# A two-layer attention trunk on one core: the first operands of the input projections turned operand by operand between the first products, and spread factors turned by halves

## The chip, the cores and the metric

The kernel runs on one core of a Trainium2 chip. The metric is the device time of one execution in microseconds (us), taken as the median of several runs. TensorE multiplies and transposes, VectorE (DVE) and ScalarE (ACT) move and combine tiles, GpSimd (POOL) does elementwise work too and issues some DMAs, SyncE (SP) issues most of them. The engines meet only through semaphores.

## The reference

`x` has 2048 tokens of 1024 float32 values. Two layers follow each other, each with an RMS norm ahead and a residual addition behind, and a last RMS norm ends the trunk:

```python
for layer in range(DEPTH):                       # DEPTH = 2
    h = rms_norm(x, norm_g[layer])
    if layer % 2 == 0:
        u = h @ w_in_even[i]                     # 1024 x 3328
        aq, ak, av, ag, bq, bk, bv, bg = jnp.split(u, even_splits, axis=-1)
        a_out = diff_attention(...)              # 4 heads, two softmax maps each, causal by chunks of 64
        b_out = swa_sink_attention(...)          # 8 heads, window of 128, a sink per head
        mixed = jnp.concatenate([a_out * silu(ag), b_out * silu(bg)], axis=-1)
        y = mixed @ w_out_even[i]
    else:
        u = h @ w_in_odd[i]                      # 1024 x 4096
        c_out = chunk_attention(...)             # 16 heads, own chunk and the 8 before it
        y = (c_out * silu(cg)) @ w_out_odd[i]
    x = x + y
return rms_norm(x, final_g)
```

## The kernel before

The program is a row of stages with a barrier of all engines between them: `p0` (input projection of the even layer), `a` (differential attention), `b` (window attention), `o0` (output projection), `p1`, `c`, `o1` for the odd layer. Names in rows begin with the stage's letter; `p_` and `o_` stand for both projections. `share`, `share_low` and `p_operands` hold operands of the products.

**Input projection (`project`, L111).** It multiplies with seven products in place of eight (a Strassen-Winograd scheme). The 2048 tokens are taken in two passes of 1024, the columns in slabs of 256: 13 slabs in `p0`, 16 in `p1`; a pass and a slab make a group `e` of seven products, one for each operand A11, S2, S1, A12, S3, A22, S4. Each product is 12 matmuls of 128x512, since each factor is a high part (rounded, float32r) and a low part (the rest), and three of the four combinations are kept. A group writes four output blocks `n`.

A pass's operands come from four *pairs* `q` of token tiles, a pair being two tiles of 128 tokens by 1024 values. For each pair and operand (28 in all) TensorE turns a 128x512 piece by four 128x128 transposes (L967) into one of four PSUM banks used in turn, ACT writes the high part (`high`, L525), DVE the low part (`low`, L698), and only then is the bank free for the turn four places on. Four operands are sums that POOL makes (`sums_of`, L322: S1, S2, S3, S4; in `p1` DVE makes S1). In `p0` each tile is normalised first: ACT squares, DVE takes mean, inverse and scales (`mean_pair`, `invert_pair`, `scale_one`). The order of the *head*, that is of the first pass, is written out by pairs: all seven operands of pair 0, then pair 1, and so on. `HEAD` is the order inside a pair, `turn_at` the place of a turn in it. Products begin after all 28 turns.

The eight tiles of the head have six places: four in `x_buf`, and tiles 4 and 5 in the second buffer of raw weights, `raws[1]` (`LENT`); tiles 6 and 7 wait on SP until the first pair is turned. So the second slab of weights is loaded once pair 2 is turned (POOL, L287). POOL also makes the sums and low parts of the weights (L291 to L315; for group 1 DVE makes the low parts, `low_weights`, L779, while group 0 runs).

In a group, ACT copies the first product out (`first_sum`, L595), DVE adds products (`near_sum` L879, `full_out` L894, L911, L927, L935), ACT rounds the result (`leave`, L557), DVE writes the rest or the gate (`second`, L831, L834), and SP stores both. Product 3 waits for `first_sum`, product 4 for `near_sum`, product 6 for the second `full_out`. In the last group SP also issues loads for the next stage between its stores (`FirstAhead`, L1100, 6 DMAs; `BandAhead`, L1128, 4 DMAs).

**Attention `a` and `c`.** DVE takes a row's extreme over logits plus bias, ACT the exponential. Its first such step in `a` waits for all of the bias table of four heads: loaded by one DMA, and filled by POOL (L1250 to L1254), which first clears the semaphores of the stage before. In `c` the first step waits for heads 0 and 1, ahead of which POOL clears semaphores, loads four heads' bias and fills all of it (L1685 to L1697).

**Output projection (`output`).** For each of 16 token tiles TensorE spreads the softmax factors over tokens by eight 128x128 transposes into `o_spread` (`spreads`, L2043), DVE multiplies (`o_gated`, `o_mix`), and 48 matmuls follow (L2058). The spreads of tile t+1 stand ahead of the matmuls of tile t.

## Time and profile before

| | us |
|---|---|
| median of 3 runs | 2610.31 |
| runs | 2606.55 to 2610.37 |
| profiled execution, its own time | 2609.58 |
| its span in the trace | 2607.7 |
| PE, DVE, ACT, POOL busy | 2402.8, 1527.7, 1143.3, 1067.1 |
| mean granted clock of TensorE | 0.97 of full speed |

A row of the trace gives start, duration, engine, line and operation, `out<-in`, shape and count; in brackets the idle time ahead of it and what ended it. PEld is TensorE's weight load. A matmul's own duration is longer than its share of the pipeline, so what a run of matmuls costs is read from start to start.

### The profile page before, as it was taken

The page shows a single profiled execution, that of the slowest core. Times are in us where ns is not written, and L with a number is a line of the kernel's source. Part 1 is how long each engine was busy: PE and PEld are TensorE (multiplying, and loading weights), DVE is VectorE, ACT ScalarE, POOL GpSimd, SP SyncE. Part 2 cuts the span into 40 slices and gives each one's busy share as a digit, 9 for nine tenths or more (in the row PEclk, how much of TensorE's full clock was granted, in tenths as well). Part 3 has the DMA queues.
Part 4 walks back from the last instruction along what each step waited for, and adds up shares of the span by engine and source line. Part 5 has one row for each costly group of instructions (what it writes and reads, how often), then busy time and mean ns, then how long its engine had stood idle before and what let it go on. Part 6 is the DMA issues. An engine that isn't in the chain of part 4 may idle for free. (4 is left out here: it accounts for less than half of the span.)

```text
span 2607.7 us, 45783 instructions
## 1 busy us (share of the span) xinstructions
PE 2402.8 (92%) x17560; PEld 1992.4 (76%) x17560; DVE 1527.7 (59%) x2877; ACT 1143.3 (44%) x2400; POOL 1067.1 (41%) x838
## 2 busy tenths in 40 slices
PE   5999999997999998889969999899997999998998
PEld 4777778875777876678858888788886788887887
DVE  6444665435888886756544422744323788887555
ACT  4333343334777775612233333433332666665221
POOL 5677768771000002210057877678774201100000
PEclk7999999997999999989989999999999999999999
DMA  2555434457464224556434544344433463453452
GB/s 105 168 187 182 150 120 157 143 165 174 102 142 112 57 98 131 162 194 244 166 111 154 173 118 142 117 146 158 138 104 111 158 199 129 146 171 111 152 203 81
DMA packets 221367, 376.72 MB, mean 144 GB/s; under 512 B 54964, under 2 KB 108896, under 8 KB 220128
## 3 DMA queue, kind: packets, MB, share of 16 engines
q1 hardware_dynamic: 200816, 299.35, 35.9%
q0 software_dynamic: 18992, 72.36, 9.2%
q8 instruction: 141, 2.31, 0.4%
q10 hardware_dynamic: 1344, 2.10, 0.3%
q14 instruction: 74, 0.61, 0.1%
HBM read 236.33 MB, written 142.90 MB: 145 GB/s over the span
## 5 line engine op out<-in xcount | busy, mean ns | idle before, releaser
L1052 PE MATMUL p_acc<-p_operands,p_w_hi 128*128 128x512 f32 x1600 | 611.4, 393 | 8.8 <-DVE p_full_out L911 8.6
L291 POOL TENSOR_TENSOR p_w_lo<-p_w_raw,p_w_hi 128x512 fp32r<-128x512 f32 x240 | 333.1, 1396 | 157.0 <-ACT p_w_hi L543 156.3
L1052 PE MATMUL p_acc<-share,p_w_hi 128*128 128x512 f32 x1024 | 384.0, 395 | 10.0 <-DVE p_full_out L911 6.7
L1052 PEld LDWEIGHTS p_acc<-p_operands,p_w_hi 128*128 128x128 f32 x1600 | 302.1, 189 | 71.3 <-POOL p_w_raw L309 4.7
L1052 PE MATMUL p_acc<-share,p_w_lo 128*128 128x512 f32 x896 | 350.5, 391 | 0.0
L543 ACT ACTIVATE p_w_hi<-p_w_raw 128x512 fp32r<-128x512 f32 x252 | 156.4, 623 | 248.4 <-POOL p_w_raw L309 108.1
L1052 PE MATMUL p_acc<-share_low,p_w_hi 128*128 128x512 f32 x624 | 246.4, 395 | 5.9 <-DVE p_operands L698 3.1
L1052 PE MATMUL p_acc<-share_low,p_w_lo 128*128 128x512 f32 x624 | 243.3, 390 | 0.0
L1052 PEld LDWEIGHTS p_acc<-share,p_w_hi 128*128 128x128 f32 x1024 | 192.2, 189 | 51.7 <-DVE p_operands L698 5.9
L831 DVE SCALAR_TENSOR_TENSOR p_lo_out<-p_full_out,p_hi_out 128x512 fp32r<-128x512 f32 x116 | 123.4, 1064 | 178.9 <-ACT p_hi_out L557 178.9
L1833 DVE CUSTOM_DVE_ANT_0 c_prob<-c_logits,c_bias 128x640 f32<-128x640 f32 (+4 forms) x256 | 179.5, 738 | 69.5 <-PE c_logits L1748 52.0
L1864 ACT ACTIVATE c_prob<-c_prob,c_neg_max 128x640 f32<-128x640 f32 (+4 forms) x256 | 193.2, 757 | 44.6 <-DVE c_neg_max L1833 44.6
L2058 PE MATMUL o_acc<-w_out_hi,o_m_hi 128*128 128x512 f32 x512 | 203.7, 398 | 4.8 <-DVE o_m_lo L2010 4.8
L2058 PE MATMUL o_acc<-w_out_hi,o_m_lo 128*128 128x512 f32 x512 | 201.1, 393 | 0.0
L2058 PE MATMUL o_acc<-w_out_lo,o_m_hi 128*128 128x512 f32 x512 | 201.0, 393 | 0.0
L1052 PEld LDWEIGHTS p_acc<-share,p_w_lo 128*128 128x128 f32 x896 | 168.7, 188 | 35.7
L1411 ACT ACTIVATE a_prob<-a_prob,a_neg_max 128x128 f32<-128x128 f32 (+15 forms) x128 | 153.9, 1202 | 84.7 <-DVE a_neg_max L1371 83.5
L1748 PE MATMUL c_logits<-share 64*128 64x256 f32 (+2 forms) x1440 | 138.6, 323 | 32.5 <-DVE c_neg_max L1833 22.5
L894 DVE COPY p_full_out<-p_acc 128x512 f32<-128x512 f32 x58 | 40.0, 690 | 204.8 <-PE p_acc L1052 204.8
L1748 PEld LDWEIGHTS c_logits<-share 64*128 64x128 f32 x1440 | 112.2, 189 | 57.0 <-DVE c_neg_max L1833 38.9
L291 POOL TENSOR_TENSOR p_w_lo<-ready_w,p_w_hi 128x512 fp32r<-128x512 f32 x96 | 132.0, 1382 | 51.0 <-ACT p_w_hi L543 50.7
L1792 PE MATMUL c_o<-c_prob_t,c_v 128*64 128x128 f32 x2240 | 151.6, 279 | 0.1
(248 smaller groups left out, 4806.2 us busy)
## 6 DMA issues: line engine op xcount, KB each, us to landing
scr_qh<-p_hi_out SPq DMA_DIRECT2D x116, 256.0 KB, 2.4
scr_ql<-p_lo_out SPq DMA_DIRECT2D x116, 256.0 KB, 2.6
p_w_raw<-in_w_in_even POOLq DMA_DIRECT2D x26, 1024.0 KB, 7.4
scr_gt<-p_hi_out SPq DMA_DIRECT2D x128, 128.0 KB, 2.0
ready_w<-in_w_in_odd POOLq DMA_DIRECT2D x16, 1024.0 KB, 7.0
p_w_raw<-in_w_in_odd POOLq DMA_DIRECT2D x16, 1024.0 KB, 6.8
share<-scr_qh SPq DMA_DIRECT2D x28, 512.0 KB, 9.1
share<-scr_ql SPq DMA_DIRECT2D x28, 512.0 KB, 10.4
```

Of the source, the lines that this page charges most:

```text
L291: nc.gpsimd.tensor_tensor(w_lo[:, k, :, :], w_source(e, k), w_hi[:, k, :, :].bitcast(F32), ALU.subtract).then_inc(w_made, 1)
L543: nc.scalar.activation(w_hi[:, k, :, :], w_source(e, k), ACT.Copy).then_inc(w_cast, 1)
L831: nc.vector.scalar_tensor_tensor(out=lo_out[:, buf, :], in0=full_out[:, buf, :], scalar=factor, in1=hi_out[:, buf, :].bitcast(F32), op0=AL ...
L894: nc.vector.tensor_copy(full_out[:, n % 2, :], x[:, :]).then_inc(taken, 1)
L1052: last = nc.tensor.matmul(bank[:, :], wt[:, k, c, :], at[k][:, c, :], start=starts and step == 0, stop=step == 3 * HK - 1, skip_group_chec ...
L1411: nc.scalar.activation(p, p, ACT.Exp, bias=neg_max[:, j:j + 1], scale=-1.0, accum_out=row_sum[:, g % 2, m:m + 1]).then_inc(exp_done, 1)
L1748: last = nc.tensor.matmul(logits[half][:, lo:hi], q_sb[b][x][rows, i * P:(i + 1) * P], k_sb[kb][y][rows, tile * P:tile * P + hi - lo], sta ...
L1792: last = nc.tensor.matmul(o_ps[half * HD:(half + 1) * HD, at:at + P], v, prob_t[:, s % 2, t, half, :], start=t == 0, stop=t == w - 1)
L1833: nc.vector.tensor_tensor_reduce(out=prob[:, j, 0:n + SPARE], in0=logits[half][:, END - n:END + SPARE], in1=bias[:, b, WIDE - n:WIDE + SPARE],
L1864: nc.scalar.activation(p, p, ACT.Exp, bias=neg_max[:, j:j + 1], scale=-1.0, accum_out=sums[:, 2 * hp + half, i:i + 1]).then_inc(exp_done, 1)
L2058: last = nc.tensor.matmul(acc[u % 4][:, :], mt[:, t % 2, c, :], wt[:, c, half * BLK:(half + 1) * BLK], start=step == 0, stop=step == 3 * K ...
```

## The change

1. **Heads operand by operand.** The turns of the first pass go by operands (`ORDER`), four pairs each, and the seven products of group 0 stand between them: A11, S2, product 0, S1, product 1, A12, product 2, A22, product 3, S3, product 4, S4, products 5 and 6. DVE, ACT and POOL follow in that order; sums get places of their own, tiles 6 and 7 lie in `hi_out` and `lo_out` (`LAID`) and are loaded at once. Group 0's weight work, results and the weights of group 1 are written out between the operands.
2. **Weights of group 1** are loaded by POOL after the last sum of the head.
3. **Loads ahead** move from SP, between the last stores, to POOL, which has nothing else then.
4. **Masks.** In `a`, head 0's bias is loaded and filled first and the semaphores are cleared last; in `c` likewise for the first two heads.
5. **Spreads by halves.** Each 128x128 transpose becomes two of 64 rows (64x128 weights, 64 moving columns), which DVE reads through a rearranged view.

```diff
-        HEAD = (A11, S1, A12, S2, S3, A22, S4)
+        ORDER = (A11, S2, S1, A12, A22, S3, S4)
...
         def slot_of(b):
-            return b % 2 if b in (6, 7) else b % XS
+            return b % XS
...
+            if b in LAID:
+                return (hi_out, lo_out)[b - LAID[0]][:, :, :].bitcast(F32).rearrange("p a b -> p (a b)")
...
             if q < PAIRS:
-                return 7 * q + HEAD.index(o)
+                return PAIRS * ORDER.index(o) + q
...
             for q in range(PAIRS):
-                sums_of(q)
-                if q == LENT[0] // 2:
-                    pool.wait_ge(x_turned, 7 * (q + 1))
-                    load_weights(1)
-                if q == 0:
+                if norm:
+                    head_first(q)
+                if q == (2 if norm else 0):
                     first_weights(0)
-                if q == 1:
-                    more_weights(0)
+                head_second(q)
+            more_weights(0)
+            for q in range(PAIRS):
+                head_third(q)
             third_weights(0)
+            for q in range(PAIRS):
+                head_fourth(q)
+            pool.wait_ge(pool_sums, SUMS)
+            pool.wait_ge(x_turned, turn_at(LENT[0] // 2, A22) + 1)
+            load_weights(1)
             last_weights(0)
...
+            for sem in stored_a + stored_b:
+                pool.wait_ge(sem, 16 * 2 * N)
+            for free, load in ahead.loads():
+                pool.wait_ge(mm_done, 7 * (G - 1) + free)
+                load(pool)
...
-                    if e == G - 1:
-                        for free, load in ahead.loads(n % 4):
-                            sp.wait_ge(mm_done, 7 * e + free)
-                            for sem in stored_a + stored_b:
-                                sp.wait_ge(sem, 16 * 2 * N)
-                            load(sp)
...
+                if n < 2:
+                    act.wait_ge(pool_sums, SUMS)
+                    act.wait_ge(x_turned, turn_at(PAIRS - 1, A22) + 1)
...
+            high_head(A22)
+            leave(0)
+            high_head(S3)
+            cast_weights(0, 5)
+            cast_weights(0, 6)
+            high_head(S4)
+            leave(1)
+            for k in range(3):
+                cast_weights(1, k)
+            leave(2)
+            for k in range(3, 7):
+                cast_weights(1, k)
+            leave(3)
...
+            low_head(S4)
+            second(1)
+            for k in range(3):
+                low_weights(k)
...
+            second(2)
+            for k in range(3, 7):
+                low_weights(k)
...
-            for q in range(PAIRS):
-                turn_head(q)
-            for e in range(G):
+            turn_head(A11)
+            turn_head(S2)
+            for k in range(5):
+                product(0, k)
+                turn_head(ORDER[k + 2])
+            product(0, 5)
+            product(0, 6)
+            for e in range(1, G):
...
-            dve.wait_ge(mask_set, 3)
             for g in range(G + 3):
+                if g == 0:
+                    dve.wait_ge(mask_set, 2)
+                if g == TPB:
+                    dve.wait_ge(mask_set, 6)
...
                 for c in range(KC):
-                    last = nc.tensor.transpose(spread[:, c, :], post.wide[:, t % 2, c, :], keep["ident"][:, :])
+                    for r in range(2):
+                        rows = slice(r * HD, (r + 1) * HD)
+                        last = nc.tensor.transpose(spread[:, r, c * HD:(c + 1) * HD], post.wide[rows, t % 2, c, :], keep["ident"][rows, rows])
```

TensorE at the end of the head of `p0`, before: the last turns of pair 3, then the products of group 0 (`x4` and `x8` are one and two turns).

```order
L967 MATMUL p_acc<-keep_ident,p_f 128x128 x4
L967 MATMUL p_acc<-keep_ident,p_x 128x128 x4
L967 MATMUL p_turned<-keep_ident,p_f 128x128 x4
L967 MATMUL p_turned<-keep_ident,p_x 128x128 x4
L967 MATMUL p_acc<-keep_ident,p_x 128x128 x8
L1052 MATMUL p_acc<-share_low,p_w_hi 128x512
L1052 MATMUL p_acc<-p_operands,p_w_hi 128x512
L1052 MATMUL p_acc<-share_low,p_w_lo 128x512
```

And now, from the last third of product 0 on: four turns of S1 (whose sums lie in `near_sum`, `far_sum` and `full_out`), then product 1.

```order
L1092 MATMUL p_acc<-share_low,p_w_hi 128x512
L1092 MATMUL p_acc<-p_operands,p_w_hi 128x512
L1092 MATMUL p_acc<-share_low,p_w_lo 128x512
L1008 MATMUL p_turned<-keep_ident,p_near_sum 128x128 x4
L1008 MATMUL p_turned<-keep_ident,p_far_sum 128x128 x4
L1008 MATMUL p_acc<-keep_ident,p_full_out 128x128 x8
L1092 MATMUL p_acc<-share_low,p_w_hi 128x512
L1092 MATMUL p_acc<-p_operands,p_w_hi 128x512
L1092 MATMUL p_acc<-share_low,p_w_lo 128x512
```

What moved: 20 of the 28 turns now stand behind product 0, in fours.

ACT in `p0` around group 0, before: the copy of product 0, group 0's last weights, group 1's weights with the results between them, and group 1's first copy (last row).

```order
L595 ACTIVATE p_first_sum<-p_acc 128x512 [waits p0_mm_done]
L543 ACTIVATE p_w_hi<-p_w_raw 128x512 [waits p0_w_made,w_loaded0] x2
L543 ACTIVATE p_w_hi<-p_w_raw 128x512 [waits w_loaded0]
L543 ACTIVATE p_w_hi<-p_w_raw 128x512 [waits p0_mm_done,w_loaded4]
L543 ACTIVATE p_w_hi<-p_t 128x512 [waits p0_mm_done,p0_w_made,w_loaded4]
L543 ACTIVATE p_w_hi<-p_w_raw 128x512 [waits p0_mm_done,p0_w_made,w_loaded4]
L557 ACTIVATE p_hi_out<-p_full_out 128x512 [waits p0_taken]
```

And now, from the end of A22's high parts: `leave(0)`, S3, two weights, S4, `leave(1)`, then group 1's weights.

```order
L590 ACTIVATE p_hi_out<-p_full_out 128x512 [waits p0_taken,p0_x_turned,p0_pool_sums]
L555 ACTIVATE share_low<-p_turned 128x4x128 [waits p0_x_turned] x2
L555 ACTIVATE share_low<-p_acc 128x4x128 [waits p0_x_turned] x2
L573 ACTIVATE p_w_hi<-p_w_raw 128x512 [waits p0_w_made,w_loaded0]
L573 ACTIVATE p_w_hi<-p_w_raw 128x512 [waits w_loaded0]
L555 ACTIVATE p_operands<-p_turned 128x4x128 [waits p0_x_turned] x2
L555 ACTIVATE p_operands<-p_acc 128x4x128 [waits p0_x_turned] x2
L590 ACTIVATE p_hi_out<-p_full_out 128x512 [waits p0_taken,p0_x_turned,p0_pool_sums]
L573 ACTIVATE p_w_hi<-p_w_raw 128x512 [waits p0_mm_done,w_loaded4]
L573 ACTIVATE p_w_hi<-p_t 128x512 [waits p0_mm_done,p0_w_made,w_loaded4]
```

What moved: the first result leaves ahead of the last two operands, and group 1's weights come after them instead of while group 0's first products run.

## Rows read from the trace of the kernel before

**Rows 1.** The page, part 1: busy time, share and instructions of each engine.
```profile
PE 2402.8 (92%) x17560; PEld 1992.4 (76%) x17560; DVE 1527.7 (59%) x2877; ACT 1143.3 (44%) x2400; POOL 1067.1 (41%) x838
```
**Rows 2.** Windows: length; PE, PEld, DVE, ACT, POOL busy; granted clock, DMA share, GB/s.
```profile
56.80:81.60 24.80, 21.21 (x88) 17.11 (x86) 9.36 (x15) 8.60 (x16) 14.47 (x11) 0.93 0.28 85
...
1317.00:1323.50 6.50, 5.34 (x33) 4.54 (x34) 4.96 (x8) 3.78 (x7) 4.18 (x3) 0.80 0.84 320
1348.60:1374.30 25.70, 22.08 (x88) 17.79 (x87) 10.18 (x17) 8.66 (x16) 14.46 (x11) 0.87 0.26 83
```
**Rows 3.** Timeline, head of p0: normalising, parts and sums.
```profile
9.45 2.48 DVE L681 SCALAR_TENSOR_TENSOR p_x<-p_x,p_inv,p_g 128x1024 f32<-128x1024 f32 x2
...
24.35 1.15 DVE L80 TENSOR_TENSOR p_root<-p_root,p_mean 128x2 f32<-128x2 f32 x1
...
31.57 0.60 ACT L525 ACTIVATE share_low<-p_turned 128x512 fp32r<-128x512 f32 x1 [7.01 <-PE p_turned L967]
...
32.20 0.69 DVE L698 TENSOR_TENSOR p_operands<-p_turned,share_low 128x512 fp32r<-128x512 f32 x1 [2.96 <-ACT share_low L525]
...
51.92 1.27 POOL L336 TENSOR_TENSOR p_f<-p_f,p_x 128x512 f32<-128x512 f32 x1
```
**Rows 4.** Timeline, head of p1: two whole turns that follow each other.
```profile
1322.97 0.60 PE L967 MATMUL p_acc<-keep_ident,p_x 128*128 128x128 f32 x4
1323.41 0.60 PE L967 MATMUL p_turned<-keep_ident,p_f 128*128 128x128 f32 x4
```
**Rows 5.** Timeline, TensorE's wait in group 0 of p0 and of p1.
```profile
76.98 1.08 PE L1052 MATMUL p_acc<-p_operands,p_w_hi 128*128 128x512 f32 x2 [3.59 <-DVE p_full_out L911]
...
1368.81 0.77 PE L1052 MATMUL p_acc<-share,p_w_hi 128*128 128x512 f32 x1 [3.62 <-DVE p_full_out L911]
```
**Rows 6.** Timeline, end of p0 and start of a.
```profile
606.16 1.23 SPq L1100 DMA_DIRECT2D share_low<-scr_qh  x2
...
607.03 0.69 DVE L834 TENSOR_TENSOR p_hi_out<-p_full_out,p_lo_out 128x512 f32<-128x512 f32 x1 [0.78 <-ACT p_lo_out L559]
...
608.74 1.07 SPq L451 DMA_DIRECT2D scr_gt<-p_hi_out  x2
...
615.77 1.08 PE L1277 MATMUL a_logits<-share_low 128*128 128x128 f32 x4 [10.24 <-PEq L120]
```
**Rows 7.** Timeline, end of p1 and start of c.
```profile
2003.75 0.69 DVE L935 TENSOR_TENSOR p_full_out<-p_acc,p_near_sum 128x512 f32<-128x512 f32 x1 [0.41 <-PE p_acc L1052]
2009.23 0.63 ACT L559 ACTIVATE p_lo_out<-p_full_out 128x512 f32<-128x512 f32 x1 [6.62 <-DMA scr_gt<-p_hi_out]
...
2013.50 0.90 PE L1748 MATMUL c_logits<-share 64*128 64x128 f32 x6 [9.79 <-PEq L120]
```
**Rows 8.** The page, part 6: DMA issues, KB each, us to landing.
```profile
p_w_raw<-in_w_in_even POOLq DMA_DIRECT2D x26, 1024.0 KB, 7.4
scr_gt<-p_hi_out SPq DMA_DIRECT2D x128, 128.0 KB, 2.0
```
**Rows 9.** Timeline: first steps of a, a wait for loads in a, first steps of c.
```profile
622.01 0.29 DVE L1371 CUSTOM_DVE_ANT_0 a_prob<-a_logits,a_bias 128x128 f32<-128x128 f32 x1 [14.29 <-POOL a_bias L1254]
...
630.34 1.54 PE L1277 MATMUL a_logits<-share_low 128*128 128x512 f32 x4 [1.56 <-DMA ready_v<-scr_v_a]
...
2016.02 1.44 POOL L1685 DMA_DIRECT2D c_bias<-scr_skew_c  x2 [26.94 <-issue]
...
2023.24 0.29 DVE L1833 CUSTOM_DVE_ANT_0 c_prob<-c_logits,c_bias 128x128 f32<-128x128 f32 x1 [12.66 <-POOL c_bias L1690]
```
**Rows 10.** The chain that ended last: start, length, what; two pieces of 33.
```profile
2424.31 0.87 PE o_spread L2043 x8
2425.18 10.93 PE o_acc L2058 x48
```
**Rows 11.** Half transposes in a: their weight loads by tile; one row of the timeline.
```profile
L1287 PEld LDWEIGHTS a_turned<-keep_ident,a_prob x552: 134/138/143, 700.2 to 880.0; 64*128 64x128 f32 x184
...
680.00 0.71 PE L1287 MATMUL a_turned<-keep_ident,a_prob 64*128 64x64 f32 x16
```

More of the change, by code:

```diff
@@ L721, in early_first_sums @@
                     q = PAIRS + side
-                    a11, a12, a21, a22 = halves_of(q)
+                    a11, a12, a21, a22 = (cube(half) for half in halves_of(q))
                     arrived(dve, 2 * q)
@@ L729, in early_second_sums @@
                     q = PAIRS + side
-                    a11, a12, a21, a22 = halves_of(q)
+                    a11, a12, a21, a22 = (cube(half) for half in halves_of(q))
                     dve.wait_ge(dve_sums, DS + 1 + side)
@@ L741, in early_fourth_sums @@
                     q = PAIRS + side
-                    a11, a12, a21, a22 = halves_of(q)
+                    a11, a12, a21, a22 = (cube(half) for half in halves_of(q))
                     dve.wait_ge(x_turned, turn_at(q, A12) + 1)
@@ L749, in late_sums @@
                     q = PAIRS + 2 + side
-                    a11, a12, a21, a22 = halves_of(q)
+                    a11, a12, a21, a22 = (cube(half) for half in halves_of(q))
                     dve.wait_ge(half_loaded["a21"], 32)
@@ L757, in late_sums @@
                     q = PAIRS + 2 + side
-                    a11, a12, a21, a22 = halves_of(q)
+                    a11, a12, a21, a22 = (cube(half) for half in halves_of(q))
                     dve.wait_ge(half_loaded["a11"], 32)
@@ L771, in late_fourth_sums @@
                     q = PAIRS + 2 + side
-                    a11, a12, a21, a22 = halves_of(q)
+                    a11, a12, a21, a22 = (cube(half) for half in halves_of(q))
                     dve.wait_ge(x_turned, turn_at(q, A12) + 1)
@@ L862, in _ @@
-            for e in range(G):
+                for q in range(PAIRS):
+                    mean_pair(q)
+                    invert_pair(q)
+                    scale_one(2 * q)
+                    scale_one(2 * q + 1)
+                low_head(A11)
+            else:
+                for q in range(PAIRS):
+                    first_sum_of(q)
+                    low(q, A11)
+            low_head(S2)
+            low_head(S1)
+            x, y, z, w = acc[0:4]
+            dve.wait_ge(mm_done, 2)
@@ new lines, in _ @@
+            dve.wait_ge(copied, 1)
+            nc.vector.tensor_tensor(near_sum[:, :], y[:, :], first_sum[:, :], ALU.add).then_inc(taken, 1)
+            low_head(A12)
+            low_head(A22)
+            dve.wait_ge(mm_done, 4)
+            nc.vector.tensor_copy(full_out[:, 0, :], x[:, :]).then_inc(taken, 1)
+            low_head(S3)
+            second(0)
+            dve.wait_ge(mm_done, 5)
+            nc.vector.tensor_tensor(far_sum[:, :], y[:, :], first_sum[:, :], ALU.add).then_inc(taken, 1)
@@ L863, in _ @@
+            dve.wait_ge(mm_done, 7)
+            room(3)
+            nc.vector.tensor_tensor(full_out[:, 1, :], z[:, :], near_sum[:, :], ALU.add).then_inc(taken, 1)
+            second(3)
+            for e in range(1, G):
                 p, s = divmod(e, N)
@@ L938, in _ @@
                 second(n + 3)
-                if e == 0:
-                    low_weights(6)
                 if last:
@@ L1109, in queries, with loads @@
             self.load(eng, part, 0, far, slice(3, 6, 2))
-    def loads(self, n):
-        return {0: [(2, self.keys)], 3: [(6, self.queries)]}.get(n, [])
+    def loads(self):
+        return [(2, self.keys), (6, self.queries)]
 class BandAhead:
@@ L1670, in _ @@
         def _(pool):
-            st.clear_before(pool)
+            if ready is not None:
+                st.clear_before(pool)
             masks = [0]
```

229 lines of the change are left out of this document (109 added, 120 removed).

## The prediction

> **What bounds the kernel now.** I read the page first: TensorE is busy for 2402.8 of 2607.7 us [rows 1], so a gain must take work off TensorE or close one of its gaps, some 200 us in all. Most groups of products run without one. The list of waits and the timeline then show where the gaps of this change lie: both heads, the two barriers behind the projections, and the first steps behind these barriers. In p0 products begin at 56.8 and group 0 ends at 81.6; in p1 (start 1316.7, stage times from there) products begin at 31.9 and group 0 ends at 57.6 [rows 2]. Both groups hold a gap of 3.6 us ahead of product 6, for DVE's second `full_out` [rows 5], and a time at the low level of the clock, so they take 24.8 and 25.7 us. At the end the chain is TensorE alone: 0.87 us of spreads and 10.9 us of matmuls per token tile [rows 10].
>
> **Unit costs.** 48 matmuls in 10.93 us give 2.72 us for a product of 12 at the full clock (2.4 GHz) [rows 10]. A turn takes 0.44 us from start to start [rows 4], at 1.2 GHz twice that. Its high part takes ACT 0.60, its low part DVE 0.69, a sum POOL 1.27 [rows 3]. So an operand's four turns and a product take TensorE 1.76 + 2.72 = 4.5 us, and ACT needs 2.4, DVE 2.8, POOL at most 5.1 for it: TensorE sets the pace once POOL is ahead.
>
> **Head of p0, up to product 0.** All eight tiles are now normalised first. DVE ends the first pair at 11.93 [rows 3]. A further pair costs 2.48 for scaling, five small steps of about 0.2 alone or 1.15 beside POOL [rows 3], of which I take half as slow (3.4), and 0.7 for mean and root: 6.6. Three pairs end at 31.7. S2 of the last pair needs one more sum and turn; at the low clock four turns take 3.5 us, so product 0 starts at about 35.8.
>
> **From product 0 to the end of group 0.** Seven products are 19.0 us and twenty turns 8.8. Between them one wait remains: S3's high parts stand behind `leave(0)` on ACT, and that behind product 3 and its copy by DVE. After product 3 come the copy 0.7, leave 0.6, four high parts 2.4 and a low part 0.7, that is 4.4 us, while the turns of S3 cover 1.8: 2.6 us of idle TensorE ahead of product 4. `leave(0)` also waits for all sums. POOL has 16 of them and eight weight steps before, at 1.27 each, and comes to the same time (54 us against 54), so that wait costs nothing here, but there is little slack. Sum 30.4 us. For the clock I add 1.0 at the first products and 1.2 behind the wait: half of what 5 us at 1.2 GHz cost. Group 0 ends at 68.5.
>
> **Group 1.** The second slab's load moves behind the last sum, about 54.9 in place of 49.6; it lands within 7.4 us [rows 8] at 62, early enough. But ACT and DVE take group 1's weights only after S4. In before they did it while group 0's products ran. Counted from the end of group 0: DVE's first low part at -1.8, POOL's three sums to +2.1, ACT's and DVE's parts 1 to 3 to +5.5, POOL's last sum +6.8, parts 4 to 6 on DVE +8.8, the fourth result +9.5, its leave +10.2, then group 1's `first_sum` +10.8. Product 3 of group 1 is due at 3 x 2.72 = +8.2 and waits for that copy: 2.6 us, with 0.7 for the clock 3.3. This is the gap that takes the place of the 3.6 us before. So p0 gains 81.6 - 68.5 - 3.3 = 9.8.
>
> **Head of p1.** Six tiles of 0.52 MB are loaded in one go. At the 320 GB/s of the early stretch [rows 2] they take 9.8 us; POOL's sums of S2 behind that end at 11.3, the turn at 12.3. Then 30.4, clock 2.7, group 1's 3.3: 48.7 against 57.6, a gain of 8.9. Both heads 18.7. Bounds: with neither the clock's share nor the wait in group 1, about 30; with 1.2 GHz through all of group 0, about 0.
>
> **Loads ahead on POOL.** At the end of p0 two loads of the next stage stand ahead of the last store on SP: the gate is ready at 607.7, its stores are issued up to 609.8, and stage a starts at 615.77 [rows 6]. Now the stores go out at once: 607.7 + 1.1 issue + 2.0 landing [rows 8] + 0.3 = 611.1, a gain of 4.6. In p1 the last result lies ready at 2004.44, but ACT waits for an earlier store until 2009.23 [rows 7]. Without that: 2004.5 + 0.63 + 0.69 + 1.1 + 2.0 + 0.5 = 2009.5 against 2013.5, a gain of 4.0. POOL has been idle there for 26 us [rows 9], which covers its issues. Bounds 0 (the loads land late or slow the stores as before) and 5 each.
>
> **Masks.** In c POOL's bias load starts 2.5 us after the barrier [rows 7, 9], behind clearing; that goes, and one DMA instead of two stands ahead of the first step. I take 3.0 (2.5 to 5). In a the first step moves from 6.2 to some 3.5 us after the start, but TensorE then waits at +14.6 for loads that SP issues from the start on, already 1.56 us now [rows 9]. The gain is a longer wait there: 0 (at most 2.7).
>
> **Spreads.** Eight whole transposes cost 0.87 us [rows 10]. Sixteen halves of the same form take 0.71 us in a, end to end [rows 11]. 32 tiles x 0.16 = 5.1 us, all on TensorE's path. Bounds 0 and 8. DVE's read by a rearranged view lies under 10.9 us of matmuls. The rows show that half loads overlap: one lasts 138 ns [rows 11], and sixteen would make 2.2 us. The Trainium skill (TensorE: Matmul & The Clock Gate, LDWEIGHTS) gives a weight load P/1.2 ns for its P columns, whatever the number of rows, so that a half costs as much as a whole. By it, one after the other, sixteen would take 1.71 us and the kernel some 2606 us, an estimate from that page. Rows 11 speak against that, if this place is like a's.
>
> **Sum.** 18.7 + 4.6 + 4.0 + 3.0 + 5.1 = 35.4. Profiled execution 2609.6 - 35.4 = 2574.2; its time lies 0.7 below the median, so I forecast 2575.
>
> **Rivals.**
> (a) *The clock stays low through group 0.* TensorE's turns leave it busy but in small pieces; before, it fell to 1.2 GHz behind gaps like the 3.6 us [rows 5]. Seven products at 5.4 in place of 2.7 are 19 us per head, of which waits absorb half: 2575 + 19 = 2594. Against it: turns and products leave almost no gap. 0.08.
> (b) *Group 1 does not wait*, because DVE and ACT get their steps done earlier than I count: 2 x 3.3 less, 2568. 0.12.
> (c) *Loads ahead take the stores' place.* Now from another queue they use the same 16 engines; if the stores land no earlier, 8.6 us are lost: 2584. For it: DMA is the wait in rows 7. Against it: stores land in 2.0 us while POOL's weights are loaded all the time [rows 8]. 0.10.
> (d) *Half loads don't overlap* in the spreads (other neighbours than in a): 16 x 0.138 = 2.21 us a tile, 1.34 more than now, 43 us: 2609.6 - 30.3 + 43 = 2622, slower than before. It decides from 1.8 us a tile, 114 ns a half. Rows 11 show 44. 0.02. The Trainium skill's rule above (TensorE: Matmul & The Clock Gate, LDWEIGHTS), at some 2606 us, has another 0.02.
> (e) *The change isn't what it says:* the order of instructions shows turns and products interleaved, so this is only that the gain is given back later, as POOL, which is behind after the head, delays group 2. Its first low part comes at +12.7 and TensorE needs the second at +24.4; it is on time by 7 us. If not, some 10 us are lost: 2585. 0.04.
>
> **How the numbers follow.** The forecast as it stands has 0.62; (b), (c) and (e) lie inside or at the edge of its own bounds. Range 2561 to 2592: at the low end heads of 26 and spreads of 8 with both full barriers, at the high end (c) with heads of 10. It leaves out (a) in part, (d) and the ends, 0.18. A measurement of this kernel tells about 0.2% (5 us) from no change. Faster by more 0.95 (all but (d) and a rest), within it 0.03, slower 0.02.
>
> **What would show it.** First product of p0 at 36 (33 to 39), group 0's end at 68 and p1's at 45; an idle TensorE of 2 to 3 us ahead of product 4 of group 0 ended by DVE's low part of S3, and another ahead of product 3 of group 1 ended by ACT's `first_sum`, none ahead of product 6. Stage a starts some 5 us and stage c some 4 us nearer to the last product; no load stands ahead of the last store. In c the first step comes under 7.5 us after the start, and in a the wait for `ready_v` grows to 4 us. A tile of the output takes 11.6 in place of 11.8 us. It would be wrong if products ran at 0.43 us from start to start in the heads, or if a tile of the output took over 11.8.

## The result and the profile after

The changed kernel takes 2592.72 us (median of 4 runs, 2587.02 to 2594.20), the kernel before beside it 2610.34 us: a ratio of 0.9931, with a 95% interval of 0.9917 to 0.9944. That is 17.6 us less. The prediction was 2575 us, a gain of 35.4, and its range ended at 2592: right in sign, twice too large in size. The profiled execution took 2594.2 us, its span is 2592.4, against 2607.7: 15.3 us less.

Where the 15.3 us come from is read by setting the starts of the stages in the two traces side by side (before, after):

| stretch | before | after | gain | predicted |
|---|---|---|---|---|
| p0, start to its last product's end | 605.5 | 598.7 | 6.8 | 9.8 |
| from there to the first product of a | 10.2 | 9.4 | 0.9 | 4.6 |
| a and b, to the first spread of o0 | 495.9 | 495.6 | 0.3 | 0 |
| o0, first spread to the start of p1 | 205.2 | 202.6 | 2.6 | 2.6 |
| p1, start to its last product's end | 686.9 | 682.8 | 4.0 | 8.9 |
| from there to the first product of c | 9.8 | 8.5 | 1.3 | 4.0 |
| c and o1, to the last product | 586.5 | 587.0 | -0.5 | 5.5 |

Single rows are less certain than the sum. A second trace of the same changed kernel (after_again) has 601.5 for p0, 682.3 for p1 and 581.8 for c and o1, with the other rows within 0.4 us. So the heads' share in p0 and the loss in the last row are uncertain by 3 and 5 us.

The page, part 1, answers to [rows 1]: TensorE is busy for 10 us less, though it has 256 instructions more.
```profile
PE 2392.8 (92%) x17816; PEld 1976.5 (76%) x17816; DVE 1521.9 (59%) x2877; ACT 1139.5 (44%) x2400; POOL 1072.5 (41%) x853
```
The windows answer to [rows 2] (columns as there): group 0 with its turns between the products, then group 1, in p0 and in p1.
```profile
35.75:68.23 32.48, 29.70 (x167) 25.41 (x165) 18.98 (x30) 15.02 (x29) 23.23 (x20) 0.95 0.29 98
68.23:92.42 24.19, 20.94 (x85) 16.75 (x84) 10.76 (x16) 8.97 (x16) 14.90 (x12) 0.93 0.43 130
1321.76:1354.90 33.14, 30.36 (x167) 26.01 (x166) 19.36 (x30) 15.15 (x30) 22.38 (x19) 0.94 0.30 96
1354.90:1379.00 24.10, 20.84 (x86) 16.64 (x85) 10.80 (x16) 8.96 (x16) 14.80 (x12) 0.93 0.36 110
```
TensorE's timeline of both heads (start, length, what, the idle time before it and what ended it) answers to [rows 5].
```profile
35.75 0.48 PE L1092 MATMUL p_acc<-share_low,p_w_hi 128*128 128x512 f32 x1
...
56.79 0.80 PE L1092 MATMUL p_acc<-share_low,p_w_hi 128*128 128x512 f32 x1 [2.78 <-DVE p_operands L735]
...
79.85 0.51 PE L1092 MATMUL p_acc<-share_low,p_w_hi 128*128 128x512 f32 x1 [3.25 <-ACT p_first_sum L636]
...
1306.33 1.09 PE L1008 MATMUL p_turned<-keep_ident,ready_x 128*128 128x128 f32 x4 [7.74 <-PEq L1958]
...
1317.58 1.12 PE L1008 MATMUL p_acc<-keep_ident,p_lo_out 128*128 128x128 f32 x4 [1.41 <-DMA p_lo_out<-scr_xn]
...
1321.76 1.09 PE L1092 MATMUL p_acc<-share,p_w_hi 128*128 128x512 f32 x2
...
1366.41 0.47 PE L1092 MATMUL p_acc<-share,p_w_hi 128*128 128x512 f32 x1 [3.26 <-ACT p_first_sum L636]
```
In p0 product 0 begins at 35.75 and group 0 ends at 68.23 (forecast 35.8 and 68.5), with the forecast wait of 2.8 us ahead of product 4. The second wait, ahead of product 3 of group 1, is there too, but it costs more than its 3.25 us: group 1 takes 24.19 us where seven products at the full clock take 19.0, so 5.2 in all. The granted clock falls to 1.2 GHz behind the wait: eight matmuls start 0.43 us apart in place of 0.23. This is not the same in every execution: of eleven traces of kernels with this group 1, eight lose 1.8 us in this way in p0, after_again and m_both 0.1, l_last 2.8.

The barriers and first steps answer to [rows 6, 7, 9]. The first fence is the end of p0 and start of a, the second the end of p1 and start of c.
```profile
596.32 1.19 POOL L1145 DMA_DIRECT2D share_low<-scr_qh  x2 [8.80 <-PE p_acc L1092]
597.50 1.19 POOL L1145 DMA_DIRECT2D share_low<-scr_ql  x2
601.46 0.63 ACT L592 ACTIVATE p_lo_out<-p_full_out 128x512 f32<-128x512 f32 x1 [3.82 <-DMA scr_gt<-p_hi_out]
608.12 1.09 PE L1325 MATMUL a_logits<-share_low 128*128 128x128 f32 x4 [9.38 <-PEq L120]
...
623.00 1.54 PE L1325 MATMUL a_logits<-share_low 128*128 128x512 f32 x4 [5.75 <-DMA ready_v<-scr_v_a]
```
```profile
1991.30 0.63 ACT L592 ACTIVATE p_lo_out<-p_full_out 128x512 f32<-128x512 f32 x1 [5.32 <-DMA scr_gt<-p_hi_out]
1997.65 0.91 PE L1806 MATMUL c_logits<-share 64*128 64x128 f32 x6 [8.50 <-PEq L120]
1998.05 0.71 POOL L1740 DMA_DIRECT2D c_bias<-scr_skew_c  x1 [14.29 <-POOLq L120]
...
2005.87 0.20 POOL L1745 MEMSET c_bias<- 64x128 f32 x1 [6.11 <-DMA c_bias<-scr_skew_c]
2006.10 0.29 DVE L1891 CUSTOM_DVE_ANT_0 c_prob<-c_logits,c_bias 128x128 f32<-128x128 f32 x1 [11.37 <-POOL c_bias L1745]
```
ACT now waits for a store in p0 as well, 3.82 us, where before DVE's last result was the wait. And the chain that ended last, beside [rows 10]: the spreads are shorter by 0.23 us, the matmuls behind them longer by 0.20.
```profile
2421.09 0.64 PE o_spread L2105 x16
2421.74 11.10 PE o_acc L2120 x48
```

### The profile page after: what moved, and what is told of

Same layout as the page of the kernel before. It is cut to its first block and busy times, and to the rows that moved or that the text cites. A ratio compares the mean times of both kernels' runs of the same rounds, so it can differ in the third digit from the quotient of the medians.

```text
span 2592.4 us, 46314 instructions
## 1 busy us (share of the span) xinstructions
PE 2392.8 (92%) x17816; PEld 1976.5 (76%) x17816; DVE 1521.9 (59%) x2877; ACT 1139.5 (44%) x2400; POOL 1072.5 (41%) x853
## 5 line engine op out<-in xcount | busy, mean ns | idle before, releaser
L1092 PE MATMUL p_acc<-share_low,p_w_hi 128*128 128x512 f32 x624 | 248.8, 399 | 11.5 <-DVE p_operands L735 6.1
## 6 DMA issues: line engine op xcount, KB each, us to landing
share<-scr_ql SPq DMA_DIRECT2D x28, 512.0 KB, 10.2
```

What stands on the lines that cost most here:

```text
L1092: last = nc.tensor.matmul(bank[:, :], wt[:, k, c, :], at[k][:, c, :], start=starts and step == 0, stop=step == 3 * HK - 1, skip_group_chec ...
```

## The experiments

Times are medians. Where a kernel has only one execution, its trace is read and not its time. Two traces of the same kernel differ by some us in a stage (above), so waits and single stretches are compared, not ends.

### The spreads

Four kernels, each with one edit of the loop that turns the factors.
```diff
 s_whole: the loop, the PSUM tile and DVE's read as before the change
 s_half_twice (from the changed kernel), s_whole_twice (from the kernel before):
+                for again in range(2):
                     for c in range(KC):
                         ...
 s_half_rows:
-                for c in range(KC):
-                    for r in range(2):
+                for r in range(2):
+                    for c in range(KC):
```


> The changed kernel with the spreads of the output turned whole again (8 transposes of 128x128 a tile), all else as changed. Theory A (the halves gain almost nothing, because what they save in their own burst is given back at its two ends, where a matmul of the whole array stands beside a load of half of it): a tile takes 11.775 in place of 11.747 us, 32 tiles make 0.9 us, the kernel takes 2593.6 us. Theory B (the term of the prediction, 0.16 us a tile, holds, and something else in the output took it back): 5.1 us more, 2597.8 us.

> The changed kernel with the sixteen half transposes of every tile issued twice in a row (the second set writes the same values to the same place). Theory A (a fixed cost at the two ends of the burst, cheap halves inside): the second set costs only its own 16 x 0.040 = 0.64 us, so a tile of the output takes 11.75 + 0.64 = 12.39 us. Rival (each half costs what the whole tile's difference says, (11.747 - 10.90) / 16 = 0.053 us): 11.75 + 0.85 = 12.60 us.

> The kernel before with the eight whole transposes of every tile issued twice in a row. Both theories: a whole transpose costs 0.109 us inside the burst and there is nothing fixed at the ends, so a tile takes 11.775 + 0.87 = 12.65 us. If it comes out lower than 12.6, whole transposes have a fixed part too, and the comparison with the halves has to be made over.

> The changed kernel with the sixteen halves in another order: the eight of tokens 0 to 63 first, then the eight of tokens 64 to 127, so that neighbours load the same 64 rows of the array instead of taking turns. If halves overlap only because they take turns between the two halves of the rows, the burst grows to at least 16 x 0.109 = 1.74 us and a tile takes some 12.8 us. If not, 11.75 us as before.

The chains of s_whole, s_half_twice, s_whole_twice and s_half_rows, one tile of each (start, length, what):
```profile
2471.47 0.87 PE o_spread L2101 x8
2472.34 10.90 PE o_acc L2116 x48
```
```profile
2485.07 1.14 PE o_spread L2106 x32
2486.21 11.12 PE o_acc L2121 x48
```
```profile
2489.34 1.75 PE o_spread L2044 x16
2491.08 10.90 PE o_acc L2059 x48
```
```profile
2481.26 0.94 PE o_spread L2105 x16
2482.21 11.10 PE o_acc L2120 x48
```
s_whole took 2596.34 us (ratio 0.9945, 0.9931 to 0.9958; the changed kernel 0.9931): the difference of 3.6 us has an uncertainty of about its own size and decides nothing between 0.9 and 5.1. The chains do. Sixteen more halves add 1.14 - 0.64 = 0.50 us, 31 ns each; eight more wholes add 0.88, 110 ns each. So inside the burst the halves are cheaper than either theory had it, and cheaper than the wholes by 0.38 us a tile. But a tile with halves takes 11.75 us, of which 48 matmuls at 0.227 are 10.89 and the halves 0.50: 0.36 us are left that more halves don't add to. A tile with wholes is 11.77 = 10.89 + 0.88, nothing left. That the 0.36 sits at the two ends, most of it at the first, is read from the neighbours of one burst (PEld is the weight load), the changed kernel first, then the kernel before:
```profile
2420.70 0.39 PE L2120 MATMUL o_acc<-w_out_lo,o_m_hi 128*128 128x512 f32 x1
2421.02 0.58 PEld L2105 LDWEIGHTS o_spread<-keep_ident,post_wide 64*128 64x128 f32 x16 [0.35 <-issue]
2421.02 0.71 PE L2105 MATMUL o_spread<-keep_ident,post_wide 64*128 64x64 f32 x16
...
2421.67 0.50 PE L2120 MATMUL o_acc<-w_out_hi,o_m_hi 128*128 128x512 f32 x1
```
```profile
2435.72 0.39 PE L2058 MATMUL o_acc<-w_out_lo,o_m_hi 128*128 128x512 f32 x1
2435.72 1.02 PEld L2043 LDWEIGHTS o_spread<-keep_ident,post_wide 128*128 128x128 f32 x8
2435.95 1.03 PE L2043 MATMUL o_spread<-keep_ident,post_wide 128*128 128x128 f32 x8
...
2436.74 0.48 PE L2058 MATMUL o_acc<-w_out_hi,o_m_hi 128*128 128x512 f32 x1
```
Before, the first load runs with the last matmul (both at 2435.72). Now it starts 0.32 us after it, when that matmul is nearly through. From that last matmul to the first one behind the burst it is 1.02 before and 0.97 now. The Trainium skill (TensorEngine Tiling (Array Packing), Key Properties) says it in one line: changing the tiling mode drains TensorE. The traces agree, in that the first load of the burst starts late; the 0.36 us for the pair of changes is measured here. The Trainium skill's figure for a load (TensorE: Matmul & The Clock Gate, LDWEIGHTS), P/1.2 ns for P columns whatever the rows, gives 107 ns for these loads of 128 columns, an estimate from that page. The whole ones agree, with 110 ns each; as a price of a half it does not hold here: 31 ns, alternating. Grouped by rows (s_half_rows) the sixteen take 0.94 in place of 0.64 us, 0.30 us more and not the 1.1 that the expectation had at least, so taking turns between the two halves of the rows is a part of what makes them cheap, not all.

The stretch behind the first spread of o0 is shorter by 1.5 us, which the sum did not have. There nothing stands beside the burst, the clock is at 1.2 GHz, and it lies on the chain: 1.12 us against 1.94 before and in s_whole.
```profile
1103.69 1.12 PE L2105 MATMUL o_spread<-keep_ident,post_wide 64*128 64x64 f32 x16 [5.74 <-PEq L1603]
```
```profile
1111.63 1.94 PE L2043 MATMUL o_spread<-keep_ident,post_wide 128*128 128x128 f32 x8 [5.75 <-PEq L1549]
```
From there to the first product of the output it takes 6.4 us in the changed kernel and in h_copy_early, l_on_sp and h_leave, 7.9 in s_whole, heads_only and before. So the halves are worth 32 x 0.03 + 1.4 = some 2.3 us, not 5.1.

### The heads alone, and group 1

heads_only is the changed kernel with the old loads ahead, masks and spreads, that is the heads alone.

> The kernel before with the new heads of both projections alone: loads ahead on SP, masks of a and c and the spreads as before. From the trace of the changed kernel the heads gave 6.8 us in p0 and 4.0 us in p1, so 2610.3 - 10.8 = 2599.5 us. By the prediction's terms it would be 18.7 us, 2591.6 us. If the later loads had a share in the heads' gain, it comes out over 2602 us.

It took 2599.37 us (ratio 0.9955, 0.9940 to 0.9970), 11.5 us less than the kernel before measured beside it (2610.88). The heads are worth 11, not 18.7, and the other parts together some 6.

h_copy_early and h_leave move steps of ACT and DVE in group 1:
```diff
 h_copy_early, ACT:
             leave(2)
+            <first_sum of group 1>
             for k in range(3, 7):
                 cast_weights(1, k)
             leave(3)
-            <first_sum of group 1>
 h_copy_early, DVE:
             <full_out of the last result of group 0>
+            <near_sum of group 1>
             second(3)
-            <near_sum of group 1>
 h_leave, ACT, on top of it:
                 cast_weights(2, 0)
+                leave(4)
                 cast_weights(2, 1)
                 cast_weights(2, 2)
-                leave(4)
```


> The changed kernel with ACT's first_sum of group 1 moved ahead of the last four weight casts and of leave(3), and DVE's near_sum of group 1 moved ahead of the last low part, nothing else. Theory (that copy's place alone makes the 3.3 us wait and the 2.0 us at 1.2 GHz behind it, in each projection): no wait ahead of product 3 of group 1, group 1 of p0 takes 19.1 in place of 24.4 us, and with up to 1.5 us given back in groups 2 and 3 it is 7 to 10 us in all: 2583 to 2586 us. Rival (the weights of group 1 are late too, and take the wait's place at products 4 to 6): under 3 us, 2590 us or more.

> h_copy_early with ACT's leave of the first result of group 1 moved ahead of the casts of group 2's second and third parts, which wait for POOL. Theory (the deficit of group 1 is this order: a cast that waits for POOL stands ahead of a leave on ACT, the leave holds a buffer, the buffer holds DVE's next result and that product 6): the 2.9 us ahead of product 6 of group 1 go in both projections, with the clock behind them 3 to 5 us each, and 0 to 1.5 us come back in groups 2 and 3 of p0: 2581 to 2586 us. Rival (POOL's parts for group 2 are late whatever ACT does): the wait moves to the products 1 to 5 of group 2, 2590 us.

TensorE's waits in groups 1 and 2 of p0, first of h_copy_early, then of h_leave:
```profile
80.58 0.47 PE L1099 MATMUL p_acc<-share_low,p_w_hi 128*128 128x512 f32 x1 [0.54 <-DVE p_near_sum L920]
89.21 0.70 PE L1099 MATMUL p_acc<-p_operands,p_w_hi 128*128 128x512 f32 x2 [2.94 <-DVE p_full_out L966]
```
```profile
80.01 0.47 PE L1101 MATMUL p_acc<-share_low,p_w_hi 128*128 128x512 f32 x1 [0.52 <-DVE p_near_sum L922]
100.08 0.47 PE L1101 MATMUL p_acc<-share_low,p_w_hi 128*128 128x512 f32 x1 [3.50 <-ACT p_first_sum L639]
```
2590.65 us (0.9921, 0.9906 to 0.9936) and 2588.70 us (0.9931, 0.9917 to 0.9944): no gain that can be told from the changed kernel. The wait for `first_sum` goes, and comes back ahead of product 6 of group 1; taken away there, it comes back in group 2. Behind h_copy_early's wait of 2.94 us the clock stays at 2.4 GHz (matmuls 0.23 us apart), so its group 1 is 1.1 us shorter than the changed kernel's (23.1 for 24.2), but its group 2 is 1.0 longer (20.2 for 19.2). A wait of TensorE in group 4 that all of them have (0.35 to 0.40 us, for `first_sum`) ends at 141.13 us in the changed kernel, at 141.79 and at 141.12 in these two. So ACT's order is not what holds groups 1 to 3 back; both expectations fell, and the rival of h_leave stood. What holds is one step further up: POOL has the weight sums, and it waited. POOL's timeline of the changed kernel:
```profile
66.36 1.28 POOL L397 TENSOR_TENSOR p_w_raw<-p_w_raw 128x512 f32<-128x512 f32 x1 [5.92 <-DVE p_w_lo L813]
```
POOL is idle for 5.9 us, since it may overwrite the first part of group 1's weights only when DVE's low part of it is done; and this stands behind ACT's `leave(1)` and DVE's `second(1)`, though the slab landed at some 60 us. w_first moves that one pair of steps:
```diff
 ACT:
             cast_weights(0, 6)
+            cast_weights(1, 0)
             high_head(S4)
             leave(1)
-            for k in range(3):
+            for k in range(1, 3):
                 cast_weights(1, k)
 DVE:
             second(0)
+            low_weights(0)
             dve.wait_ge(mm_done, 5)
             ...
             second(1)
-            for k in range(3):
+            for k in range(1, 3):
                 low_weights(k)
```


> The changed kernel with the first weight part of group 1 taken early: ACT's cast of it stands ahead of the high parts of S4 (behind leave(1) before), DVE's low part of it ahead of far_sum. Nothing else is moved. Theory (POOL's chain of weight sums, which waits for that low part until 66.36 us, sets groups 1 to 3): POOL's first sum of group 1 starts at 62 us, and in p0 the wait of TensorE ahead of product 3 of group 1 shrinks from 3.25 to under 1 us and the step ACT first_sum of group 4, now at 140.4, comes 3 to 4 us earlier. Rival (ACT's and DVE's own steps set it): the waits and the 140.4 us stay within 1 us.

> h_leave and w_first together: first part of group 1's weights early, first_sum and near_sum of group 1 ahead of the last parts, the first leave of group 1 ahead of the casts that wait for POOL. Theory (with POOL's chain 4.5 us earlier nothing stands in the way of groups 1 to 3): the waits of 3.5 us (p0) and 2.45 us (p1) ahead of product 3 of group 2 in h_leave shrink to under 1 us, and with the clock behind them 3 to 5 us come in each head against h_leave's 2588.7: 2580 to 2583 us. Rival: no more than h_leave, 2588 us.

> w_first timed. By its trace it gains 4.2 us in p0 and about 5 in p1 against the changed kernel: 2592.7 - 9 = 2584 us, a ratio of about 0.990 to the kernel before. If part of it is lost behind p0 and p1, 2588 us or more.

> The changed kernel once more, beside w_first. 2592.7 us as before. In stage c the stalls of TensorE over 0.7 us that end with nothing visible made 4.3 us in its first trace; if they come and go by execution they are another number here (0 to 3 us), if they belong to this kernel they are again about 4 us at the same places.

POOL of w_first, and two windows of the timed one (most of group 0, whose end is at 68.95, then the 20 us up to the end of group 1):
```profile
61.60 1.27 POOL L397 TENSOR_TENSOR p_w_raw<-p_w_raw 128x512 f32<-128x512 f32 x1 [1.39 <-DVE p_w_lo L814]
```
```profile
35.60:68.00 32.40, 29.61 (x162) 25.30 (x161) 20.57 (x33) 16.28 (x31) 25.35 (x21) 0.95 0.29 95
68.00:88.00 20.00, 20.00 (x89) 16.52 (x89) 8.46 (x13) 7.36 (x14) 11.92 (x9) 1.00 0.53 164
```
The one execution of w_first took 2585.61 us. In group 1 TensorE is busy without a gap and at 2.4 GHz (in p1 too, no wait for `first_sum` is left), and the wait in group 4 ends at 137.03 (137.71 in the timed trace) in place of 141.13. (In thirteen traces whose first groups are as in the changed kernel, or differ only by the moves of h_copy_early and h_leave, this moment lies between 139.3 and 142.2, so 137 is outside their spread.) w_first_timed took 2583.67 us, ratio 0.9896 (0.9883 to 0.9909), beside it the changed kernel 2591.97 us, 0.9928 (0.9915 to 0.9941). The ranges of the two do not touch (2582.80 to 2584.98, and 2587.30 to 2595.65). So 8.3 us come from two steps moved, where the moves of h_copy_early and h_leave gave nothing that can be told. w_all, w_first with the two other moves, took 2590.23 us (0.9929, 0.9915 to 0.9942): there ACT waits 2.40 us for the first product of group 1 to copy it, the casts behind that come later, and POOL with them (its fourth sum at 72.79, in w_first at 70.00), and a wait of 2.83 us comes back in group 2. The moves that looked like the cure cost what the real one gives.

### The start of p1

In p_two two of the six tile loads are issued by ACT's queue in place of SP's.

> The changed kernel in which two of the six tile loads at the start of p1 (the last two) are issued by ACT's queue at the same moment, in place of behind the other four on SP. In the changed kernel the last tile lands 11.2 us after the start and product 0 begins at 15.4. If the issue from one queue keeps the loads below 320 GB/s, the last tile lands at 9.8 and product 0 begins at about 14. If the 16 engines are the limit, both stay within 0.3 us.

Nothing moved for the better: product 0 begins 15.7 us after the start (1321.5 - 1305.8), where the changed kernel has 15.4. Between 1305.8 and 1317.0 both traces have the same 282 GB/s. TensorE's last wait for a tile ends 10.5 us after the start; with one queue it is 11.2 in the changed kernel's trace and 10.4 in after_again. So a gain from the second queue is not seen, in one trace. The start of product 0 in p1 differs by execution: 13.7 to 15.7 us over sixteen traces of kernels with the new head, 15.4 and 14.6 in the two of the changed kernel itself; what differs in them is how late a tile lands.

### The loads ahead

```diff
 l_on_sp: the loads on SP again, at their places between the stores
 l_last (POOL):
                 pool.wait_ge(mm_done, 7 * (G - 1) + free)
+                if free > 2:
+                    pool.wait_ge(dve_done, seconds[4 * G])
                 load(pool)
 l_small: 1/8 of the columns of each of these loads
```


> The changed kernel with the loads ahead of a and c back on SP, at their old places among the stores. Theory (on POOL they are issued earlier and now slow the stores of the gates, so most of the gain is taken back): from the last matmul of p0 to a's first one it takes about 10.2 us again in place of 9.4, and in p1 9.8 in place of 8.5, 2 us together. By the prediction it would be 4.6 and 4.0 us later. ACT's wait for a store of a gate (3.82 us at 601.46) should be gone at the end of p0.

> The changed kernel with the later loads ahead (a's queries, all of c's) still on POOL but held back until DVE has the last result, so that no load moves while the stores of the earlier gates do. Theory (the loads delayed the stores, and by them ACT, which waits for a buffer): ACT's waits for a store (3.82 us in p0, 5.32 us in p1) go, the last result is ready at 600.6 in place of 602.8, and a and c start 2 to 4 us nearer to the last product; a part may come back as a wait for the loads in a and c. Total 2586 to 2593 us. Rival (the stores are slow by themselves, whatever is loaded): the two waits and both starts stay, 2592.7 us.

> The changed kernel whose loads ahead of a and c carry one eighth of their columns each (the first steps of a and c then compute with old data; same instructions, same queue, same moments). Theory (while these loads move, stores of the gates land late, and this takes back most of what the move to POOL gives): ACT's waits for a store (3.82 and 5.32 us) go, the last stores land 2.0 us after their issue, and from the last matmul to the first one of the next stage it takes about 5.5 us in place of 9.4 in p0 and 8.5 in p1. Rival (it is the issue on POOL, or the number of DMAs, not their bytes): both stay over 8 us.

| from the last product to the next stage's first | before | changed | l_on_sp | l_last | l_small |
|---|---|---|---|---|---|
| p0 to a, us | 10.2 | 9.4 | 10.6 | 12.3 | 5.2 |
| p1 to c, us | 9.8 | 8.5 | 9.0 | 11.6 | 5.1 |

The first product of a in l_small and in l_last:
```profile
604.92 1.09 PE L1325 MATMUL a_logits<-share_low 128*128 128x128 f32 x4 [5.25 <-PEq L120]
```
```profile
613.71 1.09 PE L1327 MATMUL a_logits<-share_low 128*128 128x128 f32 x4 [12.35 <-PEq L120]
```
l_small is the answer to whether the bytes matter: same queue, same moments, an eighth of the bytes (so a and c compute with old data there), and both barriers shrink to 5.2 and 5.1 us, close to the 5.6 that the prediction's own sum had for the end of p0 (611.1 - 605.5). They act on two paths, and the expectations knew only one, the stores. At the end of a stage each engine drains before the next stage begins (L120). SP comes to its drain when the stores have landed. POOL's drain ends less than 1 us after its own last load has landed, in the changed kernel (some 606.4) as in l_last (some 612.6). Start in us and length in ns of the drains, first of the changed kernel, then of l_last, at the end of p0:
```profile
L120 POOLq DRAIN  x1: 9633/9633/9633, 597.6 to 597.6; - x1
L120 SPq DRAIN  x1: 7/7/7, 607.8 to 607.8; - x1
```
```profile
L120 POOLq DRAIN  x1: 8082/8082/8082, 605.3 to 605.3; - x1
L120 SPq DRAIN  x1: 7/7/7, 606.3 to 606.3; - x1
```
In the changed kernel the last two stores take 4.4 us from issue to landing (1.9 in l_small), SP drains at 607.8, and a starts at 608.1. So the stores come last; but POOL's drain ends at 607.2, so that in p0 stores as quick as forecast would have given only some 0.6 us more, with the loads as they are. In p1 POOL's drain ends at 1991.4, 6 us ahead of SP's (1997.4): there it is the stores, by ACT's wait of 5.32 us for an earlier one. In l_last the last two stores land in 1.9 us, DVE has its last result 2.2 us after the last product as in the kernel before, and SP is through at 606.3, but POOL's loads, issued from 604.1 on, take 4.4 and 6.4 us to land, its drain ends at 613.4, and a starts at 613.7. So l_last does not show slow stores: it shows that loads ahead, issued late on POOL, hold the barrier themselves. In p1 it is the same (SP through at 2001.0, POOL's drain until 2007.0). Where POOL has no loads (l_on_sp) its drain lasts 3.1 and 2.3 us, in l_small 3.9 and 4.0. My expectation of 2586 to 2593 us for l_last was wrong: it took 2598.09 (0.9949, 0.9932 to 0.9965). In l_on_sp ACT's wait for a store is gone at the end of p0, as expected. The move from SP to POOL itself is worth 1.2 + 0.5 us (l_on_sp against the changed kernel, one trace). The Trainium skill (DMA: Bandwidth & Descriptors, Queues, rings and completion order) has the DMA engines serve the queues in turn, packet by packet. The traces do not show single packets; they show a store of SP issued at 598.4, in the midst of POOL's four loads, landing after 8.2 us, and in l_last stores issued just ahead of such loads landing after 1.9 us.

### The masks

m_both issues c's second bias load right behind the first.

> The changed kernel with c's second bias load issued right behind the first, as before, but still ahead of the masks and of the clearing. The first step of c began 8.45 us after the first matmul of c, though the first bias load was issued 2.1 us earlier than before. If the time from issue to landing (7.1 us) is the load's own, the first step stays at 8.4 to 8.5 us. If loading both at once helps or hurts, it moves by over 0.5 us.

TensorE's wait for c's first step was 8.07 us, against 8.11: the second load does not matter. The first is issued 2.1 us earlier after the first product than before (0.4 against 2.5), and takes 0.8 longer from issue to the fill that waits for it (7.8 against 7.0), so 1.3 us remain of the forecast 3.0; in l_on_sp against heads_only, with all else of the start alike, it is 8.18 against 9.59, that is 1.4. In a the earlier first step goes into the wait for `ready_v`, 1.56 before and 5.75 now (4 forecast).

## Why the prediction was right in sign and wrong in size

**p0 up to the end of group 0.** Right: product 0 at 35.75 for 35.8, group 0's end at 68.2 for 68.5, the wait ahead of product 4 2.8 for 2.6, none ahead of product 6. That the sum fits to 0.3 us is partly luck: the terms named for product 0 add up to 36.5 (31.7 + 1.3 + 3.5), not 35.8, and TensorE got the last scaled tile at 31.2; the 1.0 us for the clock at the first products did not come (they start 0.23 us apart), and group 0's end lies between 66.4 and 69.5 in other traces with this head.

**Group 1.** The wait and its place were forecast (2.6, now 3.25), but two terms were mis-sized. The clock behind it costs 1.9, not 0.7 (24.19 - 19.0 - 3.25). And groups 2 and 3 give 1.4 more back, with waits of 0.41 and 0.85 us in group 3 where the kernel before has 0.34: rival (e) at a seventh of its size. POOL's own steps were counted rightly (its first sum behind DVE's low part at 68.5 - 1.8 = 66.7, measured 66.36), but as given; that this start could be moved, and sets the wait, was not asked. w_first shows the difference that makes: 8.3 us.

**Head of p1.** Product 0 at +15.4, forecast +12.3, and this 3.1 us stays to the end of group 0 (+48.6 against +45.4). The six tiles took 11.2 us, not 9.8: 282 GB/s, not 320. The clock's term, 2.7 us where p0 has 2.2, was given no reason. The steps behind the last tile take 4.2 us (DVE's sum, POOL's, the turn, the two parts), and I had put 2.5: DVE's sum and the parts were left out.

**Loads ahead.** The step that failed is "a gain of 4.6" and "a gain of 4.0", of which 0.9 and 1.3 came. The sum let the stores land in 2.0 us: in p0 the last ones took 4.4, in p1 they took 2.0 but ACT still waited 5.32 us for an earlier one. And the sentence that POOL's 26 idle us cover "its issues" put at nothing what follows them: POOL's drain, 9.6 us, until its loads have landed, which in p0 ends 0.6 us before the stores. Rival (c) is most of what happened, with 0.10: it had the stores' part (the same 16 engines) and a price of 8.6 against 6.4 lost. Its argument against, that a store lands in 2.0 us while POOL's weights are loaded, was a median over the whole stage; the late stores of p0 stand beside four loads of 256 KB.

**Masks.** Right for a (nothing). In c 1.3 of 3.0: the load, now earlier, also takes longer.

**Spreads.** The step that failed is "sixteen halves of the same form take 0.71 us in a". As a length it holds (0.71 here too, at 2421.02). But it was set against 0.87 of the chain, which covers both ends of its burst, where 0.71 covers none. The sign to look for stood in the trace of before, the start of the last full matmul to the start of the next. Rival (d), that halves don't overlap, is refuted.

**Sum.** Heads 10.8 of 18.7, loads ahead 2.2 of 8.6, spreads about 2.3 of 5.1, the mask of c 1.3 of 3.0: 16.6 of 35.4. The 1.3 us that this trace has less come with something that this change does not touch: TensorE's stalls over 0.7 us that end with nothing visible ("issue") come in c alone, 2.4 us of them before and 4.3 in the changed kernel's first trace, none in its second, 0 to 2.7 in the fifteen others. What they are stays open. One of them, in the first trace:
```profile
2268.88 0.62 PE L1806 MATMUL c_logits<-share 64*128 64x256 f32 x6 [2.00 <-issue]
```
The range ended just short, at 2592, which was rival (c) with heads of 10 us: both came true, and the spreads and the mask were smaller as well. The two terms of the loads ahead had been taken near the top of their bounds (4.6 and 4.0 of 5), and the mask fell below its own lower bound of 2.5.

## What to carry to other kernels

When a stage is shortened, follow the slowest helper engine back to the moment from which it could start, not only the queue of the engine that TensorE is seen to wait for: here the visible waits were for ACT and DVE, moving their steps only moved the wait, and letting POOL start 4.8 us earlier by one pair of steps gave 8.3 us. A load ahead that is in flight while a stage's last stores go out is paid for at the barrier, whichever queue issues it: it delays the stores, and the engine that issued it drains late, so look at the drains of all engines before you name the one that holds the barrier. And price a change of form by a stretch that includes both its neighbours, start of the last old instruction to start of the next one.

## What the runs showed of the hardware

- Half transposes (64x128 loads, 64x64 out) cost 31 ns each when they alternate between the upper and the lower rows, 110 ns a whole one (s_half_twice, s_whole_twice); the alternating burst pays 0.36 us once for going to halves and back among full matmuls.
- In the same order by rows the sixteen halves cost 0.30 us more (0.94 against 0.64).
- A last store of 128 KB lands 1.9 us after its issue with next to nothing beside it (l_small), and 4.4 us behind four loads of 256 KB (changed kernel).
- POOL's drain at the end of a stage lasts 2.3 to 3.1 us without loads of its own and 7.2 to 9.6 us behind its four loads (l_on_sp, l_last, changed kernel); it can hold the barrier after SP is through.
- Two queues load six tiles no faster than one (282 GB/s each, one trace each).
- Behind a wait of 3.25 us TensorE ran at 1.2 GHz for 3.4 us before it was back at 2.4: the gap costs 5.2 us in all, 1.6 times what its row shows. Behind a wait of 2.94 us in h_copy_early it stayed at 2.4.
